# First mixer: the order of the second query tile's softmax, where its mask is added, and how its two maps are summed

## The reference

```python
s = jnp.einsum("bqhmd,bkhmd->bhmqk", q_blk, k)          # 4 heads x 2 maps, 128 queries at a time
mask = key_pos[None, :] <= q_pos[:, None]
p = jax.nn.softmax(jnp.where(mask, s, -jnp.inf), axis=-1)
w = p[:, :, 0] - lam * p[:, :, 1]                       # the two maps
o = jnp.einsum("bhqk,bkhd->bqhd", w, v)                 # then a norm over each head, times 1 - lam_init
...
r, i = sigmoid(xh @ wa + ba), sigmoid(xh @ wx + bx)     # the recurrence's gates
a = exp(-8 * r * softplus(-lam))
u = sqrt(1 - a * a) * (i * x)                           # h_t = a_t h_(t-1) + u_t
rec = h * gelu(gb)
return concatenate([attn, rec]) @ w_out
```

## Time and profile before

| | us |
|---|---|
| median of 3 runs | 2654.49 |
| lowest and highest | 2650.07, 2655.74 |
| profiled execution, its own time | 2653.67 |
| its span, first to last instruction | 2651.9 |
| mean granted clock of PE, as a share of full speed | 0.97 |

### The profile page before, as it was taken

How to read it: one execution, slowest core, us unless ns; L and a number is a source line. 1 busy time by engine, 2 the same in 40 slices (tenths; PEclk the granted TensorE clock), 3 DMA queues, 4 the chain that set the end, 5 groups by cost and what they waited for, 6 DMA issues and landing times.

```text
span 2651.9 us, 52642 instructions
## 1 busy us (share of the span) xinstructions
PE 2455.2 (93%) x24386; PEld 1586.6 (60%) x24386; DVE 616.5 (23%) x1160; ACT 380.9 (14%) x620; POOL 157.3 (6%) x145
## 2 busy tenths in 40 slices
PE   7889997899999999999998989998889799999996
PEld 5547776566666565666665678984578444434443
DVE  1730002100000010101001357632461332222223
ACT  1310102000000000000002243222231100000001
POOL 2000000000000000000000034420120000000000
PEclk9989998899999999999999989999999899999998
DMA  8773524599999999999999000032021469999995
GB/s 302 260 279 129 190 68 170 223 393 351 371 371 349 393 350 393 349 393 350 389 353 352 1 0 1 1 127 84 30 78 64 169 261 399 399 400 402 400 400 202
DMA packets 273255, 676.17 MB, mean 255 GB/s; under 512 B 5891, under 2 KB 9438, under 8 KB 268830
## 3 DMA queue, kind: packets, MB, share of 16 engines
q1 hardware_dynamic: 270624, 666.91, 66.9%
q0 software_dynamic: 2112, 6.04, 0.7%
q10 hardware_dynamic: 318, 0.10, 0.0%
HBM read 671.98 MB, written 1.05 MB: 254 GB/s over the span
## 4 chain that ended last, share of the span: by engine, by line
PE 76%; DMA 11%; DVE 6%; ACT 3%; SPq 2%; issue 1%; POOL 1%; DVEq 0%; ACTq 0%; POOLq 0%
PE ps L622 26%; PE ps L716 22%; PE ps L737 11%; DMA ring<-in_w_exp_up 11%; PE ps L805 5%; PE ps L997 3%; ACT arena L2068 2%; SPq L568 2%; PE ps L1130 1%; PE ps L1142 1%; PE ps L723 1%; PE ps L1140 1%; PE ps L699 1%; POOL arena L2541 1%; PE ps L657 1%
## 5 line engine op out<-in xcount | busy, mean ns | idle before, releaser
L716 PE MATMUL ps<-ring,arena 128*32 128x256 f32 x10752 | 591.6, 379 | 1.1 <-DVE arena L1741 1.1
L716 PEld LDWEIGHTS ps<-ring,arena 128*32 128x32 f32 x10752 | 344.4, 110 | 231.7 <-issue 8.1
L622 PE MATMUL ps<-hT,ring 128*128 128x256 f32 (+1 forms) x1792 | 446.0, 410 | 20.1 <-ACT arena L2068 7.3
L2068 ACT ACTIVATE arena<-ps 128x384 f32<-128x384 f32 (+5 forms) x312 | 165.9, 552 | 1799.9 <-PE ps L716 558.8
L622 PEld LDWEIGHTS ps<-hT,ring 128*128 128x128 f32 x1792 | 347.3, 194 | 121.9 <-issue 69.7
L737 PE MATMUL ps<-ring,arena 128*32 128x256 f32 x5376 | 300.5, 379 | 0.0
L805 PE MATMUL ps<-ring,arena 128*64 128x512 f32 x1024 | 232.1, 607 | 30.4 <-DMA ring<-in_w_exp_up 27.5
L737 PEld LDWEIGHTS ps<-ring,arena 128*32 128x32 f32 x5376 | 173.9, 110 | 115.3 <-issue 1.3
L1473 DVE TENSOR_TENSOR arena<-arena,ps 128x384 f32<-128x384 f32 x56 | 31.1, 555 | 802.7 <-ACT arena L2068 802.7
L805 PEld LDWEIGHTS ps<-ring,arena 128*64 128x64 f32 x1024 | 80.9, 140 | 178.4 <-issue 178.4
L622 PE MATMUL ps<-arena 128*128 128x128 f32 (+1 forms) x1064 | 133.4, 287 | 15.9 <-ACT arena L2068 5.1
(11 more groups left out here) (359 smaller groups left out, 1838.4 us busy)
## 6 DMA issues: line engine op xcount, KB each, us to landing
ring<-in_moe_wg SPq DMA_DIRECT2D x56, 2048.0 KB, 11.4
ring<-in_moe_wu SPq DMA_DIRECT2D x56, 2048.0 KB, 16.4
ring<-in_moe_wd SPq DMA_DIRECT2D x56, 2048.0 KB, 17.2
ring<-in_w_exp_gate SPq DMA_DIRECT2D x32, 2048.0 KB, 17.5
ring<-in_w_exp_up SPq DMA_DIRECT2D x32, 2048.0 KB, 18.8
ring<-in_w_exp_down SPq DMA_DIRECT2D x32, 2048.0 KB, 14.6
ring<-in_w_in SPq DMA_DIRECT2D x13, 2048.0 KB, 10.1
ring<-in_w_ada SPq DMA_DIRECT2D x12, 2048.0 KB, 13.6
```

The source lines that it names most:

```text
L622: last = mm(outp, l, r, start=(i == 0), stop=(i == n - 1))
L716: last = mm(flat[32 * q:32 * q + 32, S * r:S * r + S], x_[:, k, 32 * r:32 * r + 32], gu[:, :, k, q * P:(q + 1) * P], start=(k == 0), stop= ...
L2068: return nc.scalar.activation(*a, **k)
```

## The change

The mask is no longer added by DVE. In `scores`, each product is followed by one of the identity with the 128 columns of the causal mask, accumulated onto the last 128 columns of the same scores; `shifted` reduces and subtracts straight from PSUM. In `weighed`, the exponentials are no longer scaled by both reciprocals: the second map is scaled by the factor times the ratio of the two sums and added to the first in one instruction a head, and the remaining common factor is multiplied in where `squared` takes the output out of PSUM. DVE's order becomes: `shifted(1)`, `placed(0)`, the square of `a`, `weighed(1)`, the other two passes to `one_minus`, `copied(1)`, `mod_part(0)`, the polynomial, the recurrence's input, `squared(1)`, the product with the square root, `normed(1)`, scans, gate. On ACT, the square root moves from ahead of `gb_copied` to behind `gate(1)`, with one table load ahead of it and one behind, and `gelu_tanh` behind it; `mod_rows(1, 2)` and `gate(1)` come ahead of both.

```diff
--- before.py
+++ after.py
@@ -78,8 +78,8 @@
         ("grow_sum", 1), ("y2_ready", 2), ("grow_sum", 1), ("logits_ready", 1), ("rank2_sum", 1)],
     "ve_mixer1": [("eps_ready", 1), ("cols_ready", 1), ("lam_dot", 1), ("nl_ready", 1), ("qk_copied", 4),
         ("v_copied", 1), ("rope_done", 1), ("xb_copied", 1), ("xc_ready", 1), ("s_shifted", 1), ("w_ready", 1), ("log_a", 1),
-        ("wT_copied", 1), ("o_copied", 1), ("o_ms", 1), ("o_normed", 1), ("one_minus", 1), ("o_copied", 1), ("s_shifted", 1),
-        ("gelu_in", 1), ("w_ready", 1), ("wT_copied", 1), ("o_copied", 1), ("o_ms", 1), ("o_normed", 1), ("rec_ready", 1),
+        ("wT_copied", 1), ("o_copied", 1), ("o_ms", 1), ("o_normed", 1), ("s_shifted", 1), ("o_copied", 1), ("w_ready", 1),
+        ("one_minus", 1), ("wT_copied", 1), ("gelu_in", 1), ("o_copied", 1), ("o_ms", 1), ("o_normed", 1), ("rec_ready", 1),
         ("o_copied", 1), ("hTc_ready", 1),
         ("poolT_copied", 4), ("sel1_ready", 1), ("top1_diff", 1), ("rounds1_ready", 1)],
     "ve_deltanet": [("kraw", 1), ("kc_conv", 1), ("kF_ready", 1), ("vraw", 1), ("vc_conv", 1), ("g_pre", 1),
@@ -92,7 +92,7 @@
         ("grp_shift", 1), ("sel2_ready", 1), ("top2_diff", 1), ("rounds2_ready", 1)],
     "ve_end": [("result", 2)],
     "ac_mixer1": [("lam_exp", 1), ("nl_ln", 1), ("c_silu", 1), ("rg_sig", 1), ("s_exp", 1), ("o_rstd", 1), ("rg_exp", 1),
-        ("rg_sqrt", 1), ("gb_copied", 1), ("s_exp", 1), ("gelu_tanh", 1), ("rg_sig", 1), ("o_rstd", 1), ("top1_exp", 1)],
+        ("gb_copied", 1), ("s_exp", 1), ("rg_sig", 1), ("rg_sqrt", 1), ("gelu_tanh", 1), ("o_rstd", 1), ("top1_exp", 1)],
     "ac_deltanet": [("k_sq", 1), ("k_rs", 1), ("vc_ready", 1), ("ba_read", 1), ("sp_ln", 1), ("kTok_ready", 1),
         ("egc_ready", 1), ("q_sq", 1), ("q_rs", 1)],
     "ac_hgrn2": [("o_sq", 1), ("z_silu", 1), ("rs_done", 1), ("lb_exp", 1), ("hq_ready", 1), ("f_sig", 1),
@@ -905,7 +905,9 @@
                     for h in range(H):
                         last = mm(ps[:, 2 * m + h // 2, (h % 2) * S:(h % 2) * S + nk],
                                   qk[64 * m:64 * m + 64, h, qt * P:(qt + 1) * P], qk[64 * m:64 * m + 64, 4 + h, 0:nk],
-                                  start=True, stop=True)
+                                  start=True, stop=False)
+                        last = mm(ps[:, 2 * m + h // 2, (h % 2) * S + qt * P:(h % 2) * S + nk], ident, amask[:, P:2 * P],
+                                  start=False, stop=True)
                 last.then_inc(inc("scores_ready"), 1)
 
             def gates(g):
@@ -1595,13 +1597,10 @@
 
             def shifted(qt):
                 nk = P * (qt + 1)
-                mk = amask[:, P:2 * P] if qt == 0 else amask[:, :]
                 ve.wait_ge(*at("scores_ready", qt + 1))
-                for b in range(4):
-                    last = V.tensor_tensor(sc[:, 2 * b:2 * b + 2, 0:nk], bank(b, 2, S)[:, :, 0:nk], rep(mk, 2), ALU.add)
-                done(last)
-                done(V.tensor_reduce(mx, sc[:, :, 0:nk], AX.X, ALU.max))
-                done(V.tensor_tensor(sc[:, :, 0:nk], sc[:, :, 0:nk], over(mx, nk), ALU.subtract), "s_shifted")
+                raw = ps[:, 0:4, :].rearrange("p b (h n) -> p (b h) n", h=2)[:, :, 0:nk]
+                done(V.tensor_reduce(mx, raw, AX.X, ALU.max))
+                done(V.tensor_tensor(sc[:, :, 0:nk], raw, over(mx, nk), ALU.subtract), "s_shifted")
 
             def weighed(qt):
                 nk = P * (qt + 1)
@@ -1609,8 +1608,10 @@
                 done(V.tensor_reduce(smx, sc[:, :, 0:nk], AX.X, ALU.add))
                 done(V.reciprocal(rsm, smx))
                 done(V.tensor_scalar(rsm[:, 4:8], rsm[:, 4:8], lams[:, 5:6], None, ALU.mult))
-                done(V.tensor_tensor(sc[:, :, 0:nk], sc[:, :, 0:nk], over(rsm, nk), ALU.mult))
-                done(V.tensor_tensor(wts[:, :, 0:nk], sc[:, 0:4, 0:nk], sc[:, 4:8, 0:nk], ALU.add), "w_ready")
+                done(V.tensor_tensor(rsm[:, 4:8], rsm[:, 4:8], smx[:, 0:4], ALU.mult))
+                for h in range(H):
+                    last = V.scalar_tensor_tensor(wts[:, h, 0:nk], sc[:, 4 + h, 0:nk], rsm[:, 4 + h:5 + h], sc[:, h, 0:nk], ALU.mult, ALU.add)
+                done(last, "w_ready")
 
             def copied(qt):
                 ve.wait_ge(*at("wT_ready", qt + 1))
@@ -1620,7 +1621,7 @@
 
             def squared(qt):
                 ve.wait_ge(*at("o_ready", qt + 1))
-                done(V.tensor_copy(ot, bank(2, 4, P)), "o_copied")
+                done(V.tensor_tensor(ot, bank(2, 4, P), over(rsm[:, 0:4], P), ALU.mult), "o_copied")
                 done(V.tensor_tensor(osq, ot, ot, ALU.mult))
                 done(V.tensor_reduce(o4, osq, AX.X, ALU.add))
                 done(V.tensor_scalar(o4b, o4, 1.0 / P, SUB_EPS, ALU.mult, ALU.add), "o_ms")
@@ -1641,28 +1642,29 @@
             copied(0)
             squared(0)
             normed(0)
+            shifted(1)
+            placed(0)
             ve.wait_ge(*at("rg_exp", 1))
             done(V.tensor_tensor(rg_u, rg_a, rg_a, ALU.mult))
+            weighed(1)
             done(V.scalar_tensor_tensor(rg_u, rg_u, 1.0, rg_r, ALU.add, ALU.mult))
             done(V.tensor_scalar(rg_u, rg_u, -1.0, 0.0, ALU.mult, ALU.max), "one_minus")
-            placed(0)
-            shifted(1)
+            copied(1)
+            mod_part(0)
             ve.wait_ge(*at("gb_copied", 1))
             done(V.tensor_tensor(gt, gbF, gbF, ALU.mult))
             done(V.tensor_scalar(gt, gt, 0.044715, 1.0, ALU.mult, ALU.add))
             done(V.tensor_tensor(gt, gt, gbF, ALU.mult), "gelu_in")
-            weighed(1)
-            mod_part(0)
-            copied(1)
             ve.wait_ge(*at("rg_sig", 2))
             done(V.tensor_tensor(rg_i, rg_i, xc, ALU.mult))
+            squared(1)
+            ve.wait_ge(*at("rg_sqrt", 1))
             done(V.tensor_tensor(rg_u, rg_u, rg_i, ALU.mult))
+            normed(1)
             for c in range(4):
                 last = V.tensor_tensor_scan(rg_h[:, c, :], rg_a[:, c, :], rg_u[:, c, :], 0.0, ALU.mult, ALU.add)
-            done(last)
-            squared(1)
+            ve.wait_ge(*at("gelu_tanh", 1))
             done(V.scalar_tensor_tensor(gel, gel, 1.0, gbF, ALU.add, ALU.mult))
-            normed(1)
             done(V.scalar_tensor_tensor(mixT[:, 4:8, :], rg_h, 0.5, gel, ALU.mult, ALU.mult), "rec_ready")
             placed(1)
             mod_part(1)
@@ -2237,19 +2239,19 @@
             ac.wait_ge(*at("log_a", 1))
             done(act(rg_a, rg_r, ACT.Exp))
             done(act(rg_r, rg_r, ACT.Tanh), "rg_exp")
-            functions("sqrt_and_others")
-            ac.wait_ge(*at("one_minus", 1))
-            done(act(rg_u, rg_u, ACT.Sqrt), "rg_sqrt")
-            functions(EXP)
             ac.wait_ge(*at("gb_proj", 1))
             act(gbF[:, 0:2, :], bank(4, 2, S), ACT.Copy)
             done(act(gbF[:, 2:4, :], bank(5, 2, S), ACT.Copy), "gb_copied")
             exponentials(1)
             functions(SIG)
+            mod_rows(1, 2)
+            gate(1)
+            functions("sqrt_and_others")
+            ac.wait_ge(*at("one_minus", 1))
+            done(act(rg_u, rg_u, ACT.Sqrt), "rg_sqrt")
+            functions(SIG)
             ac.wait_ge(*at("gelu_in", 1))
             done(act(gel, gt, ACT.Tanh, scale=0.7978845608028654), "gelu_tanh")
-            mod_rows(1, 2)
-            gate(1)
             functions(LN)
             head_norm(1)
             mod_rows(2, 3)
```

## The result

| | before | after |
|---|---|---|
| median us (runs) | 2654.41 (7) | 2660.81 (7) |
| lowest, highest | 2650.07, 2655.74 | 2654.40, 2662.51 |
| profiled execution | 2653.67 | 2654.40 |
| ratio of the times [95%] | | 1.0029 [1.0019, 1.0038] |

The changed kernel is slower by 6.4 us at the median, 0.29%, which a measurement of this kernel can tell from no change. The forecast was 2658.5, slower by less than 0.2%. The table holds a puzzle: the profiled execution of the changed kernel took 2654.40, only 0.7 more than that of before, and the other six took 2660.07 to 2662.51. What was profiled is not what usually happens. The times in this document are medians, and the ratios are not ratios of these medians: where a kernel's times form two groups, a median can jump from one to the other, and the two can differ by some us.

What follows compares the result with a forecast made beforehand. In the first mixer, ada(2) was gated by DVE's softmax and its weights' transfer; the change makes the transfer decide. Transfer +2.3 and clock +2.3 us gave +4.6 on 2653.67 or 2654.49, taken as 2658.5, range 2651.5 to 2661.5.

Steps and rivals of the forecast that it cites:

- The price of a change of shape: PE's scores: each switch between 64-row score and 128-row identity products costs 0.21 us, bounds 0 and 0.30.
- The first rival: PE's scores: changes of shape cost nothing, ada(2) starts 4.0 us early, total 2652.0 us; chance 0.13.
- the fully exposed load: PE's scores: each change of shape costs 0.30 us with its whole load, +7.3 us, 2661.0; chance 0.17.
- The gate: Ahead of ada(2): its last weights land at 145.6, so it starts at 145.7 instead of 143.38, +2.3 us.
- eight are 6.9 and 8.6 us: PE's scores: eight score and mask pairs take 6.9 us in tile 0 and 8.6 in tile 1, from 1.71 and 2.96.
- the next transposes at 121.2: PE behind tile 1's scores: transposes start at 121.2 instead of 113.44, 7.8 us later.
- the sum: Whole kernel: +2.3 us for the transfer and +2.3 for the clock, +4.6 in all, giving 2658.3 or 2659.1.
- so the shift goes through to the end: Behind the output projection: what follows is PE's, with loads hanging on PE, so the delay stays whole to the end.
- `ada(2)`'s slow start: ada(2) begins at half clock after over 6 us of idle PE, stays there about 4.6 us and loses 2.3 us.

Runs made afterwards that it cites:

- Experiment 1: Changed kernel with all eight score products of a tile first and the eight identity products behind them; 2649.25 us, 0.9994 of before.
- experiment 3: Kernel before with only the identity products in scores() and shifted reading PSUM, old order and old weighed kept; 2661.24 us, 1.0028 of before.
- Experiment 5: Changed kernel without the transfers of the last two parts of ada(2)'s weights, all engine instructions kept; 2665.26 us, 1.0046 of before.
- experiment 2: Changed kernel with the mask added by DVE again, new order and one scaled pass kept; 2647.54 us, 0.9986 of before.
- experiment 4: Kernel before with only the one-pass sum, that is weighed() and squared() of the changed kernel; 2651.55 us, 0.9996 of before.
- experiment 6: Experiment 2 with ada(1) and the last part of gb earlier on PE, and gb's copy, square and gelu_tanh early on ACT; 2652.01 us, 1.0003 of before.
- experiment 8: Kernel before run and profiled again, unchanged; 2655.21 us, 1.0005 of before.
- experiment 9: Changed kernel with four filler products, results unread, in PE's two waits ahead of tile 1's scores; 2656.74 us, 1.0010 of before.
- experiment 7: Changed kernel run and profiled again, unchanged; 2660.65 us, 1.0030 of before.
- experiment 11: Experiment 2 with the four filler products of the first waits and eight more ahead of ada(2); 2648.51 us, 0.9980 of before.
- experiment 12: Experiment 9 with thirteen more filler products in the wait ahead of ada(2); 2657.84 us, 1.0011 of before.

## Why the prediction failed

**The price of a change of shape** was right: 0.83 and 1.04 us a pair against 0.86 and 1.07, gates at 97.11 (97.1), next transposes at 120.93 (121.2). The first rival (changes cost nothing) is out, and so is the fully exposed load. Experiment 1 shows it from the other side. The Trainium skill, TensorEngine Tiling (Array Packing), Key Properties, says that a change of tiling mode drains TensorE; the trace agrees, with 0.22 us each time.

**The gate** was right: the last issue for `ada(2)` at 132 (132.7), its start at 145.24 (145.7), PE idle for 6.3 us (over 6), half clock at its start, 2.4 us lost (2.3). DVE's marks came at 132.7 and 151.1 (133.2 and 151.6). The projection began at 156.59 (157.0), 4.3 after before's instead of 4.7. Experiments 3 and 5 confirm who waits for whom, and experiment 2 the size.

**The step that failed** is the one that reads "eight are 6.9 and 8.6 us" for tile 1, and with it "the next transposes at 121.2": it prices 8.6 us of PE work at full clock because the one profile of before showed 1.00 there. PE waits several times around the first tile's output, about 109 to 112 us, and whether the clock stays up differs between executions of the same kernel. It fell in the second profiles of both kernels (115.0 and 110.7) and in those of experiments 1, 3 and 5 (110.9, 115.1, 114.6). It did not in the first ones, nor in those of experiments 2, 4 and 6. The changed kernel has 8.4 us of scores right behind that point where before has 2.96, in front of `ada(1)` and so of the transfer, which is its gate; before waits for DVE's softmax there. So the eight pairs take 12.7 us instead of the 8.6 of the sum, and the fall costs the changed kernel 6.0 us at the projection. It costs before 0.2 (experiment 8). Only two of the changed kernel's 19 executions were profiled; that the other fourteen above 2660 had the fall as well is inferred from their times, and from experiment 9, where that group is gone.

**In numbers:** the fall explains the changed kernel's two groups, 6.0 us at the projection and 6.15 in the time. What the sum describes, an execution without it, is the smaller group: four of 19, at 2653.91 to 2654.40. The sum gave 2658.3 for it, 3.9 too much. That the forecast of 2658.5 still lies only 2.3 under the median of 2660.81 is luck: it left out the fall (6.15) and kept a loss that is mostly given back later (3.9 too much), and the two largely cancel. With fillers in both kernels the medians differ by 2656.74 - 2652.87 = 3.9 us; that this is near the sum's 4.6 confirms nothing, since experiment 9's profile got 3.4 us of its time behind 2110 us.

**"so the shift goes through to the end"** failed too: it shrank. In the first pair of profiles 4.3 us at the projection became 0.7 at the end; in the second pair (7 and 8), 8.9 became 5.1. Part of it goes early: the granted clock, 0.50 after the projection, comes back 41.9 us after the projection's start in before (194.2) and 42.3 in experiment 8, but after 37.8 us in both profiles of the changed kernel (194.4 and 200.4). The rest goes in the second block, in two stages of 64 passes. First before, then after:

```profile
1451.10 17.05 PE L622 MATMUL ps<-hT,ring 128*128 128x256 f32 x64 [5.87 <-issue]
...
1515.92 11.21 PE L622 MATMUL ps<-wba,hT 128*128 128x16 f32 x64
```

```profile
1454.44 15.47 PE L622 MATMUL ps<-hT,ring 128*128 128x256 f32 x64 [5.89 <-issue]
...
1517.69 9.58 PE L622 MATMUL ps<-wba,hT 128*128 128x16 f32 x64
```

A shift of 3.3 us at 1451 is 1.8 at 1516 and 0.1 at 1540. Experiments 7 and 8 have the same two stages with the same durations within 0.04 us: 7.5 us become 4.3. The first stage stands behind a wait of 5.9 us and in both the clock is partly at 0.50, for a shorter time in the changed kernel; what decides for how long is open. The 2.3 us that the sum took for `ada(2)`'s slow start are real at the projection and gone at the end: experiments 11 and 12 removed them and gained nothing. So the sum had one term too few and took one as kept that is given back. Before's own two groups of times (near 2649.6 and near 2655.2) stay unexplained: no execution of the first group was profiled.

**The rest of the change** is worth 6.8 us at the median (experiment 2), but only 0.14%, 3.7 us, by the ratio of all executions, with an interval from 1.3 to 6.1. Its projection starts 3.5 us earlier than the earlier trace rows. How much of it is the one-pass sum is not shown: experiment 4's 2.8 us at the median are not clear of no change.

## What to carry to other kernels

Group TensorE's products by the rows of the array that they use: here each change between 64 and 128 rows cost 0.2 us, and scores with masks in turns took 2.8 to 3.9 times as long as the scores alone. Where weights are loaded into slots that a TensorE stage frees, added TensorE work ahead of that stage delays the transfer by as much, and saving time on other engines buys nothing (experiment 3). And before pricing work behind a broken-up stretch at full clock, look at the spread of the times and at a second profile: one profile shows one of several ways in which the clock can fall.

## What was unexpected of the hardware

- The clock differs between executions of one kernel on the same work. The changed kernel's windows from 103 to 115 us have PE busy for 6.65 and 3.65 us in both profiles, yet it fell at 115.0 in one and stayed up in the other, and the runs form two groups 6 us apart, 3 and 9 of 12. What decides is open. The Trainium skill, TensorE: Matmul & The Clock Gate, has the clock follow how busy TensorE has been; the filled waits of experiment 9 agree (no fall in its profile), but these two windows show that the busy time which the profile gives does not tell the two cases apart.
- A fall behind a broken-up stretch, not an idle one, came at 115.0, while PE was working on the scores without a break since 112.1.
- A warm start of one stage (7.0 instead of 9.0 to 9.4 us) was not kept: no gain at the end, twice.
- Experiment 5 had less to load and no wait for the transfer, and was 4.6 us slower than the changed kernel at the median.
- The same 64 passes behind the same wait of 5.9 us take 15.4 to 15.5 us in some profiles and 17.1 in others (1451 us), and a second stage at 1516 us goes with them (9.5 to 9.6 or 11.2). Here, 1.3 ms behind the change, 3.2 us of its effect are lost or won.
